# The eight sample rows' projections: from 24 matmuls a weight group to column quarters and a sum

## The reference

```python
h = rmsnorm(x, ln1_g)
u, va, q, k, v = project(h, w_in[l], pos)     # one [1024, 2560] matrix, five groups of 512 columns
a_out = sgu(u, va, ...)                       # gating unit, 128-position chunks; samples: one position
b_out = dilated attention, three patterns     # prompt: 512 keys; samples: 2048 cached rows and the own one
x = x + concat(a_out, b_out) @ w_out          # [1024, 1024]
x = x + hier_moe(rmsnorm(x, ln2_g), ...)      # 32 experts, two for each row
y = rmsnorm(x, lnf_g)
```

## Time and profile before

| | us |
|---|---|
| three runs | 514.86, 517.9, 516.79 |
| median | 516.79 |
| profiled execution: span from first to last instruction | 513.3 |
| its own whole time | not given apart from the span |
| mean granted TensorE clock | 0.929 of full |
| PE busy (3278 matmuls) | 400.7 (78%) |
| PE weight loads busy | 227.7 (44%) |
| DVE busy | 306.8 (60%) |
| ACT busy | 227.5 (44%) |
| POOL busy | 91.6 (18%) |

### The profile page before, as it was taken

One profiled execution on the slowest core, in us unless ns is written; L12 is line 12 of the kernel. 1 busy time (PEld: TensorE's weight loads), 2 busy tenths in 40 slices (PEclk: granted clock), 3 DMA queues, 4 the chain that ended last, 5 costly groups with the idle time before them and its releaser, 6 DMA issues. The chain is left out here.

```text
span 513.3 us, 8474 instructions
## 1 busy us (share of the span) xinstructions
PE 400.7 (78%) x3278; PEld 227.7 (44%) x3278; DVE 306.8 (60%) x506; ACT 227.5 (44%) x395; POOL 91.6 (18%) x91
## 2 busy tenths in 40 slices
PE   0999996986999999999999998428777778777100
PEld 0454443433544455565535555316554545555000
DVE  1967568996566644454354222765776777777077
ACT  4732121333363744434233112406768686866042
POOL 0000204622401000000000001032343443423000
PEclk9999998998999999999999998558999999999755
DMA  8664306759008306300065987335999999996084
GB/s 305 232 222 162 127 0 219 275 154 338 2 2 312 101 21 231 116 1 0 1 218 208 348 296 291 117 129 195 342 327 333 355 368 361 351 335 253 31 332 166
DMA packets 39207, 104.97 MB, mean 204 GB/s; under 512 B 5656, under 2 KB 6552, under 8 KB 39168
## 3 DMA queue, kind: packets, MB, share of 16 engines
q1 hardware_dynamic: 32736, 90.00, 48.9%
q0 software_dynamic: 5856, 12.81, 6.7%
q10 hardware_dynamic: 576, 1.64, 1.0%
HBM read 97.87 MB, written 14.81 MB: 220 GB/s over the span
## 5 line engine op out<-in xcount | busy, mean ns | idle before, releaser
L1420 PE MATMUL bank<-weights_split,tokens_split 128*128 128x512 f16 (+1 forms) x840 | 194.2, 385 | 4.8 <-DVE weights_split L957 3.0
L1420 PEld LDWEIGHTS bank<-weights_split,tokens_split 128*128 128x128 f16 (+1 forms) x840 | 77.8, 97 | 110.7 <-issue 16.9
L587 POOL TENSOR_TENSOR big<-big,att 128x1536 f32<-128x1536 f32 x8 | 27.7, 3469 | 102.8 <-DMA att<-sample_q 54.2
L1656 PE MATMUL bank<-tokens_split,vring 128*128 128x64 f16 x768 | 28.9, 196 | 16.1 <-DVE vring L1306 16.1
L1306 DVE SCALAR_TENSOR_TENSOR vring<-big,vring 128x1024 f16<-128x1024 f32 x30 | 35.4, 1221 | 6.4 <-ACT vring L850 6.4
L1045 DVE TENSOR_SCALAR big<-bank,den 128x64 f32<-128x64 f32 x32 | 9.1, 284 | 48.9 <-PE bank L1476 48.9
L870 ACT ACTIVATE tokens_split<-bank 128x512 f16<-128x512 f32 x32 | 17.4, 594 | 45.0 <-PE bank L1645 45.0
L1313 DVE SCALAR_TENSOR_TENSOR tokens_split<-bank,tokens_split 128x512 f16<-128x512 f32 x32 | 20.6, 686 | 27.6 <-ACT tokens_split L870 27.6
L1656 PEld LDWEIGHTS bank<-tokens_split,vring 128*128 128x128 f16 x768 | 25.3, 100 | 19.7 <-DVE vring L1306 19.7
L603 POOL DMA_DIRECT2D h_rows<-vring x5 | 2.7, 535 | 157.8 <-DVE vring L1200 157.8
L850 ACT ACTIVATE vring<-big 128x1024 f16<-128x1024 f32 x30 | 30.2, 1069 | 0.0
(11 more groups left out here) (190 smaller groups left out, 657.2 us busy)
## 6 DMA issues: line engine op xcount, KB each, us to landing
big<-in_w_gate SPq DMA_DIRECT2D x15, 1024.0 KB, 7.2
big<-in_w_up SPq DMA_DIRECT2D x15, 1024.0 KB, 8.7
big<-in_w_down SPq DMA_DIRECT2D x15, 1024.0 KB, 10.6
vring<-in_w_in SPq DMA_DIRECT2D x12, 512.0 KB, 5.0
big<-in_cache_win_k SPq DMA_DIRECT2D x24, 256.0 KB, 3.7
vring<-in_cache_win_v SPq DMA_DIRECT2D x24, 256.0 KB, 3.6
big<-in_w_out SPq DMA_DIRECT2D x8, 512.0 KB, 7.2
big<-expert_rows SPq DMA_DIRECT2D x8, 512.0 KB, 7.4
```

What stands on the lines that cost most here:

```text
L587: nc.gpsimd.tensor_tensor(prod[:, :, :], kring[:, b % 2], qb[:, b % 2, :].unsqueeze(1).to_broadcast([P, NPAT, W]), ALU.mult).then_inc(prod ...
L1420: ins = T.matmul(out, hT[:, high_low, k, tokens], wg[:, place, part, k, columns], start=k == 0 and high_low + part == 0, stop=k == KD - 1 ...
L1656: ins = T.matmul((ptb, ovb)[q // 2][:, e * CAP:(e + 1) * CAP], esplit[q][:, part, k, :], xsplit[:, b, k, high_low, e * CAP:(e + 1) * CAP], ...
```

## The change

Three things. **The product.** The samples' turned rows get a buffer of their own, `samples_split`, for each chunk 32 columns: 8 high, 8 low, 16 of zero. `sample_part` makes a sample unit with 16 matmuls instead of 24: for two halves of four chunks, for the two weight parts, four matmuls, each of another chunk and each into another quarter of 32 partitions of one bank. ACT copies the whole bank to SBUF (`copy_part`, 128x512), and `sample_sum` adds the quarters with one float32 matmul with a constant 0/1 matrix `fold` (128x8) into another unit. The low x low term, left out before, comes with it.

**The order.** The part and the sum are units of their own in `UNITS`, and other work stands between them while ACT copies. The sum of q comes after the projection of k0, that of k after va0, that of va after v0, those of v and u in the fill list. On DVE the rope of q4 comes after that of k0; on ACT va 4 comes after the copy of v0, and `exps(0)` still after va 4. In the fill list the u4 items are gone; v's sum stands after u0, u's part after u3, its sum between value groups 4 and 5; between groups 5 and 6 stand mix 2 and 3, between 6 and 7 nothing. sgu 0 is turned after task 29, sgu 1 after 30, sgu 2 and 3 both after 31.

**The out stage.** The row tiles are normed, turned and routed in the order 0, 1, 2, 4 (samples), 3; the sample parts and sums stand beside out(2,0) and out(2,1), and tile 3 is last.

```diff
+    c[r[r % 32 < 2 * NS], C_SUM + r[r % 32 < 2 * NS] % NS] = 1
...
-UNITS = [(_kind, t) for _kind in ("q", "k", "va", "v") for t in TILES]
-UNITS += [("u", t) for t in range(NT - 1)]
-UNITS += [("mix", j) for j in range(4)]
-UNITS += [("u", NT - 1)]
-OUT_ORDER = [(0, 0), (1, 0), (0, 1), (1, 1)] + [(t, h) for t in range(2, NT) for h in range(2)]
-UNITS += [("out", 2 * t + h) for t, h in OUT_ORDER]
+UNITS = [("q", t) for t in range(NT - 1)] + [("part", "q"), ("k", 0), ("q", NT - 1)]
+UNITS += [("k", t) for t in range(1, NT - 1)] + [("part", "k"), ("va", 0), ("k", NT - 1)]
+UNITS += [("va", t) for t in range(1, NT - 1)] + [("part", "va"), ("v", 0), ("va", NT - 1)]
+UNITS += [("v", t) for t in range(1, NT - 1)] + [("part", "v"), ("u", 0), ("v", NT - 1)]
+UNITS += [("u", t) for t in range(1, NT - 1)] + [("part", "u"), ("mix", 0), ("mix", 1), ("u", NT - 1), ("mix", 2), ("mix", 3)]
+UNITS += [("out", n) for n in (0, 2, 1, 3)] + [("part", "out0"), ("out", 4), ("out", 2 * NT - 2)]
+UNITS += [("part", "out1"), ("out", 5), ("out", 2 * NT - 1), ("out", 6), ("out", 7)]
...
+ROW_ORDER = [0, 1, 2, NT - 1, 3]
...
-for _b, _rest in enumerate(([("u", 0)], [("u", 1)], [("u", 2)], [("u", 3.0)], [("u", 3.5), ("mix", 0), ("mix", 1)],
-                            [("mix", 2), ("mix", 3), ("u", 4.0)], [("u", 4.5)], [])):
+FILL += [("u", 0, part) for part in range(KD)] + [("sum", "v", 0)]
+for _b, _rest in enumerate(([("u", 1)], [("u", 2)], [("u", 3.0)], [("u", 3.5), ("part", "u"), ("mix", 0)],
+                            [("mix", 1), ("sum", "u")], [("mix", 2), ("mix", 3)], [], [])):
...
-TURN_AFTER = {20: ("att", 0), 24: ("att", 1), 27: ("sgu", 0), 28: ("att", 2),
-              29: ("sgu", 1), 30: ("sgu", 2), 31: ("sgu", 3)}
+TURN_AFTER = {20: [("att", 0)], 24: [("att", 1)], 28: [("att", 2)], 29: [("sgu", 0)], 30: [("sgu", 1)],
+              31: [("sgu", 2), ("sgu", 3)]}
...
+            def copy_part(kind, dst):
+                n = UNIT[("part", kind)]
+                act.wait_ge(acc_ready, n + 1)
+                nc.scalar.activation(dst, acc[n % 2][:, :], ACT.Copy).then_inc(free_a, 1)
...
-            for t in range(NT):
+            for t in range(NT - 1):
                 va(t)
-                if t < PIECES:
-                    split_high(3, t)
+                split_high(3, t)
+            copy_part("va", part_in)
+            copy_unit(("v", 0), vv[:, 0, :])
+            va(NT - 1)
...
             exps(0)
-            copy_unit(("v", 0), vv[:, 0, :])
...
-            rope("q", 4)
             for t in range(NT):
                 rope("k", t)
+                if t == 0:
+                    rope("q", NT - 1)
...
+            def sample_part(kind, place, half):
+                u = UNIT[("part", kind)]
+                if half == 0:
+                    free_wait(pe, u)
+                for part in range(2):
+                    for j in range(4):
+                        ins = T.matmul(acc[u % 2][32 * j:32 * j + 32, :], samples_split[:, 4 * half + j, :],
+                                       wg[:, place, part, 4 * half + j, :],
+                                       start=half + part == 0, stop=half + part == 2)
+                if half == 1:
+                    ins.then_inc(acc_ready, 1)
+
+            def sample_sum(unit, src):
+                u = UNIT[unit]
+                free_wait(pe, u)
+                T.matmul(acc[u % 2][0:NS, :], fold, src, start=True, stop=True).then_inc(acc_ready, 1)
...
-            for t in range(1, NT):
+            for t in range(1, NT - 1):
                 project(("k", t))
                 turn_qk("k", t - 1)
+            for half in range(2):
+                sample_part("k", 1, half)
+            turn_qk("k", NT - 2)
...
-            for t in range(NT):
+            for t in range(NT - 1):
                 project(("va", t))
+                if t == 0:
+                    left(pe, ("part", "k"))
+                    sample_sum(("k", NT - 1), part_in)
+            for half in range(2):
+                sample_part("va", 0, half)
             project(("v", 0))
+            left(pe, ("part", "va"))
+            sample_sum(("va", NT - 1), part_in)
...
-            for t in range(2, NT):
-                project_out(t, 0)
-                router(t - 2)
-                project_out(t, 1)
-                h2_turns(t - 1)
-            router(NT - 2)
-            h2_turns(NT - 1)
-            router(NT - 1)
+            pe.wait_ge(fin_copied, 1)
+            wait_turned_out(pe, ("sgu", NT - 1))
+            for half in range(2):
+                sample_part("out0", 1, half)
+            project_out(2, 0)
+            left(pe, ("part", "out0"))
+            sample_sum(("out", 2 * NT - 2), part_out)
+            router(0)
+            h2_turns(1)
+            for half in range(2):
+                sample_part("out1", 0, half)
+            project_out(2, 1)
+            left(pe, ("part", "out1"))
+            sample_sum(("out", 2 * NT - 1), part_out)
+            router(1)
+            h2_turns(2)
+            project_out(3, 0)
+            router(2)
+            h2_turns(NT - 1)
+            project_out(3, 1)
+            router(NT - 1)
+            h2_turns(3)
+            router(3)
```

More of the change, by code:

```diff
@@ L179, in finished_in @@
 def finished_in(n):
-    return [(kind, t) for kind, t, part in fill_of(n) if kind == "mix" or kind != "pv" and part == KD - 1]
+    done = []
+    for kind, t, part in fill_of(n):
+        if kind == "mix" or kind in ("u", "v") and part == KD - 1 or kind == "part" and part == 1:
+            done.append((kind, t))
+        elif kind == "sum":
+            done.append((t, NT - 1))
+    return done
 SPLIT_AFTER = {at + i: (group, i) for group, at in ((4, 5), (5, 13)) for i in range(PIECES)}
@@ L305, in build @@
         rtmp = cut(att, 0, W)
+        part_in = gain[:, 0:W]
+        part_out = cut(att, 1024, 512)
         vr = cut(vring, 0, 2, NPAT, W)
@@ L534, in _ @@
             down_load(sp, 3, 6)
[L535 removed]
+            sp.wait_ge(acc_ready, UNIT[("out", 7)] + 1)
             gate_up_loads(sp, 4, 8)
@@ L793, in _ @@
                 for kind, t in finished_in(n):
-                    if kind != "mix":
+                    if kind == "part":
+                        copy_part(t, part_in)
+                    elif kind != "mix":
                         copy_unit((kind, t), (vv if kind == "v" else uu)[0:rows_of(t), t, :])
@@ L799, in _ @@
                     high_v(b)
-                if n in TURN_AFTER:
-                    turn_head(*TURN_AFTER[n])
+                for head in TURN_AFTER.get(n, []):
+                    turn_head(*head)
                 if n == 5:
@@ L835, in turn_h2 @@
                     turn(("h2", 2 * t + c), h2T[:, 4 * c:4 * c + 4, 0:rows_of(t)])
-            for t in range(NT):
-                square2(t)
-                turn_h2(t)
+            for at, t in enumerate(ROW_ORDER):
+                if t == 2:
+                    copy_part("out1", part_out)
+                square2(at, t)
+                if t == 1:
+                    copy_part("out0", part_out)
+                turn_h2(at, t)
             act.wait_ge(gexp_in, 1)
@@ L1188, in _ @@
             add_out(1, 0)
-            for t in range(NT):
+            for at, t in enumerate(ROW_ORDER):
                 n = rows_of(t)
-                if t >= 2:
+                if t in (2, 3):
                     add_out(t, 0)
+                if t == 2:
+                    add_out(NT - 1, 0)
                 add_out(t, 1)
@@ L1534, in fill @@
                     return
+                if kind == "part":
+                    sample_part(t, W_ORDER.index(t) % 2, part)
+                    return
+                if kind == "sum":
+                    left(pe, ("part", t))
+                    sample_sum((t, NT - 1), part_in)
+                    return
                 if part == 0:
```

134 lines of the change are left out of this document (80 added, 54 removed).

## The result

The changed kernel takes **522.13 us** in the median of four runs (521.17 to 524.55), the kernel before beside it 517.35 (four runs, 514.86 to 519.07): a ratio of 1.0127, with a 95% interval of 1.0089 to 1.0165. It is slower by 1.3%, and "no change", the forecast, was wrong. The profiled execution took 522.43 us and its span is 520.5 (513.3 before); its mean granted clock is 0.902 (0.929). Ratios leave out disturbed runs (three of the six of "four edits, kept busy", 512.01 to 514.80), so they need not be the quotient of two medians.

A forecast was written before the change was run, and what follows sets the result against it. PE was taken as the bound from 128 to 308 us, with PE and DVE competing before. 5.45 - 3.5 - 2.0 = -0.05 on a median of 516.79 gave 517.0 us, range 511 to 522.5 (the forecast's own 514.5 to 519.5).

The forecast's parts named there:

- +5.45: Up to the attention: 2.4 for k's late sum, 2.05 for va's, 1.0 for a longer clock fall.
- -3.5: Attention, net: 12.2 us come off, 4.3 for parts and sums and 4.4 for waits come on.
- 4.4 less the 1.2 that go: Attention waits of PE: 4.4 us new (value splits, head turns, a bank); old ones of 0.8 and 0.4 vanish.
- -2.0: Out projection and router, net: -6.5 from cheaper sample units, +2.2 and +2.3 lost to waits for normed rows.
- +2.2: Out stage: tile 2's turns follow after 2.8 us of work, while unit end to normed row takes 5.05.
- 9.5: Tail: us from the last unit's end to the first routing operation, with the last full tile last; 8.1 before.
- the clock's 1.0: Up to the attention: 1.0 us added for a longer clock fall after PE's two longer waits, bounds 0 and 2.
- DVE and POOL collide more: Rival near 60 us: a split locked out by a POOL product costs +1.3 at k3, another meeting 1.7; 520, chance 0.20.
- quarters that don't overlap: Rival: narrow matmuls run one after another, 2.6 us more for each part; 529, chance 0.12.
- The waits fall well: Rival: -1.2 at k3, value stalls half hidden (-2), no longer clock fall (-1); 513, chance 0.18.
- PE bounds everything: Rival: PE is the bound throughout, so all 22.8 us saved on it come off; 494, chance 0.05.
- -0.05: Whole kernel: sum of the three stage terms, 5.45 - 3.5 - 2.0, taken as no change.

The follow-up runs named there:

- four edits, kept busy: The four edits plus useless matmuls in two TensorE waits (20 ahead of the k sum, 13 ahead of tile 3's turns): 511.43 us, ratio 0.9843.
- four edits: Changed kernel with k's sum before k3's turn, va's before v0, tile 2's turns and router one unit later, gating head 3's turn after out(1,0): 511.81 us, ratio 0.9905.
- Kept busy: Changed kernel with useless matmuls (8 and 18) filling TensorE's waits before tile 2's and tile 3's turns: 518.33 us, ratio 1.0022.
- one quarter: Changed kernel with all sixteen matmuls of a part writing to partitions 0 to 31: 533.94 us, ratio 1.0369.
- five edits: The four edits plus q's sample sum (and DVE's rope of q4) moved ahead of k0: 509.14 us, ratio 0.9851.
- va sum alone: Changed kernel with only va's sample sum moved ahead of v0, and va 4 ahead of v0's copy on ACT: 523.24 us, ratio 1.0128.
- split first: Changed kernel with POOL's first product made to wait for DVE's first split of va's weights: 524.62 us, ratio 1.0159.
- k sum early: Changed kernel with k's sample sum made before k3's turn instead of after va0: 519.09 us, ratio 1.0064.

## Why the prediction was wrong

**Up to the attention: right.** +5.45 was said, +5.8 is measured. The parts cost 0.98 (said 0.97), the sums 0.96 (1.05). The first POOL product starts at 59.93 (59.9), PE waits 7.76 before k3's turn ("nearly 8"), DVE's 8-row rope of k is done 3.7 us later (said: 2.4 and 1.0 for the clock; the low clock cost va0 another 1.2), va's sum adds 2.0 (2.05), the probabilities start at 126.9 ("near 126").

**The attention: right in kind, 1.4 too good.** -3.5 was said, -2.1 measured. The stalls have the sizes that were worked out, on PE's timeline of the changed kernel:

```profile
252.67 0.63 PE L1448 MATMUL bank<-ident,big 128*128 128x128 f32 x4 [1.56 <-DVE tokens_split L987]
```

1.56 (said 1.55), and 0.96 and 1.51 for the value splits (1.1 and 1.5). Two things were not in the sum. One is a wait for a copied probability tile, on PE's timeline of the changed kernel:

```profile
149.70 0.43 PE L1558 MATMUL bank<-big,att 128*128 128x64 f32 x2 [1.76 <-ACT att L807]
```

It was 0.61 before the change, and it is 1.75 or 1.76 in every kernel that has the change. Counted from the attention's first turn, PE came to this product 0.7 us sooner than before, and ACT's copy 0.4 later, behind an instruction (L842) that had waited for DVE; why that is later stays open. With it all waits of PE in the attention come to 5.79 us against 1.75 before, 4.0 more where the prediction had 3.2 more (4.4 less the 1.2 that go). The other is the clock after the wait of 4.00: the first 5 us of the attention ran at 1.2 GHz, and the mean over its first 9.9 us was 0.76, against 0.83 before, which is worth 0.7 us by an estimate (9.9 us times 0.07). The two make about the 1.4. In the four edits, with a wait of 2.92 there, that clock was at 1.00.

**The out stage: wrong, and this is the largest miss.** -2.0 was said, +2.3 measured. The step that failed is "+2.2" for tile 2's turns and "9.5" for the tail: both waits were found (1.8 and 4.0), both were priced at full clock. At the low clock out(3,0) cost 2.0 more, the turns 0.9 twice, the last router 1.65: 5.45 in all, and the stage without them would have been -3.1 (the way to the normed row took 4.65, not 5.05, so the waits themselves were priced a little high). Kept busy, it was 50.9, which is -2.9. I had added the clock's 1.0 to the two waits up to the attention, where rows of before showed it, and none to the waits that the change itself makes where the clock had always been high.

**The rivals.** That DVE and POOL collide more (0.20) is true of a part of the executions, and with up to +3.1 at k3's turn, not +1.3: 1.3 of delay by the locked-out split, and 1.7 for k3's unit where it ran at the low clock after a wait of 3. The profiled execution of the changed kernel had neither, so this rival isn't why that execution was slower. The quarters that don't overlap are refuted (one quarter: 3.56 for 0.98). "The waits fall well" did not happen by itself; the five edits make it happen. That PE bounds everything (494) isn't reached even by them.

**The sum.** -0.05 was said for the whole; in span it was +7.2, of which 4.3 are the out stage's miss, 1.4 the attention's, 0.35 the start's, and 1.2 the end's. That the median moved by 4.8 only is not to the prediction's credit: it carried 3.5 us from the profiled span to the median, and 1.9 of these were that the profiled execution of the kernel before was a fast one.

What stays open: the total of the va sum alone, the wait at 149.70, and the 1.2 us at the end of the changed kernel's span.

## What to carry to other kernels

Spreading a thin product over column quarters is worth what it promises, 0.98 + 0.96 us in place of 5.28, but a part, a copy and a sum is a chain through two engines, and the sum belongs in front of the next long unit, not behind it: what waits for it (here DVE's queue, then ACT's) is worth more than PE's idle microsecond. When work is taken off the bounding engine, list the waits that appear in its place and price each one twice, the wait itself and the next units at the low clock, as a range. And when a delay moves an operation of GpSimd, look which DVE operation now starts within a tenth of a microsecond of it.

## What the runs showed of the hardware

The clock's fall is not a function of the wait. k3's unit took 7.03 us after a wait of 1.92 (split first), 3.01 and 2.93, and 5.34 after 2.96 (k sum early). Two kernels with the same order and the same waits in the late attention, four edits and five edits, had the clock at 1.00 and at 0.77 from 245 to 255 us. The Trainium skill (TensorE: Matmul & The Clock Gate, Part 1: The HAM clock gate) says that the point of change depends on a phase that runs free of the kernel; these rows agree. It may also make the spread, which no run separates: in twelve runs of one kernel times lay 10.7 us apart, the longest at the lowest mean clock.

The two kernels here, 3.56 and 0.98 us for the same sixteen matmuls, give 3.6x for four column quarters. The Trainium skill (TensorE: Matmul & The Clock Gate, Measured speedup vs the span model) gives 2.38x for three column tiles; an estimate scaled from it to four is 3.2x, and the measurement is the better figure here.
